# Hybrid encoder layer: another order and other places for the input norm, the Hyena projections, the filter network and the spectra

## The chip, the cores and the metric

One core of a Trainium2 chip runs the whole layer in one launch. The metric is device microseconds of that core. TensorE is called PE here, VectorE DVE, ScalarE ACT, GpSimd POOL; SyncE (SP) issues nearly all DMAs. Each engine works through its own queue in order, and engines wait for each other with semaphores.

## What is computed

A normed input of 1024 tokens by 1024 channels is projected once, and three mixers (Hyena, RG-LRU, latent attention) share the columns. The change touches the input norm, the projection and the Hyena mixer:

```python
x = _layer_norm(x, ln_in_g, ln_in_b)
proj = x @ w_in[l]
p_hy, p_lr, p_lg, p_cq, p_ckv, p_kr = jnp.split(proj, IN_SPLITS, axis=-1)
...
u = _depthwise_conv(u, conv_w, conv_b, 1, 1)          # width 3
x1, x2, v = jnp.split(u, 3, axis=-1)
h = sin(f1 * (z @ w1 + b1)); h = sin(f2 * (h @ w2 + b2))
h = (h @ w3).reshape(length, 2, 2, 256) * window      # taps of the long filters
z = v
for o, gate in enumerate((x1, x2)):
    z = gate * (_bidir_fftconv(z, h[:, 0, o], h[:, 1, o]) + skip[o] * z)
```

Behind it stand the attention, the output projection, a norm, an expert-choice mixture of 16 experts and a last norm. All products here are float32.

## The kernel before

Everything is written out by hand: one block of code per engine, semaphores between them, and fixed word addresses in one on-chip array (`mem(at, ...)`). So the order of the work is the order of the source, and what may be loaded when follows from which buffers lie on top of each other.

The **front** runs as follows. SP loads three tiles of x (128 tokens each), then twenty small parameter loads and the window table `win`; a further tile is loaded into one of three buffers when the old one is stored and turned (L408 to L412). DVE takes statistics and norms a tile (L1454 to L1460), PE turns it with 8 transposes (`x_turn`, L983), ACT copies it with gain and offset into `xT` (L657). Between the tiles stand the filter network: two small layers (L995, L999) with DVE's argument reduction (`sine_args`, L1445 to L1450) and ACT's sine (L646), then eight tap steps (L1010) of two 64-row matmuls each, whose products DVE multiplies with the window (L1486) and POOL folds into sums and differences (L519, L520). Then PE makes the filter **spectra**: four groups of 16 matmuls with the tables `fc` and `fs` (L1026); ACT copies half of each (L683, L684) and DVE combines them (L1498 to L1502, semaphore `spectra_done`).

Next come the six Hyena **projections** of 16 matmuls (`project`, L1042). ACT applies the centre tap of the short convolution (L697), DVE the outer ones (L1515 to L1519), PE turns the result (`hy_turn`, L1054), ACT and DVE copy it (L689, L1507). DVE folds (L1535, L1536), and the **convolution** `conv(0)` begins: spectrum matmuls with `dc` and `ds` (L1077), products on DVE, inverse matmuls with `ic` and `is_` (L1087, L1088). Project 6 stands between `conv(0)` and `conv(1)`, projects 7 to 9 behind it; then PE turns Hyena's result back (L1106, semaphore `hyena_back_psum`), does project 10 and begins the RG-LRU gates (L1120), which need 16 small weights.

**SP's queue** behind the front: `win_w` chunks 0 to 2 when `fc` and `fs` have landed; the four convolution tables and `skipb` when the spectra are done; chunks 3 and 4; then, when the second convolution's inverse sums are in PSUM (`inverse_psum`), 16 loads of the attention's weights (`wq`, `wqr`, `wk`, `wv`; 128 or 256 KB each), three rope loads (1,088 KB together), chunk 5, the 16 loads of the gates' weights (16 KB each, L449), and the last chunks. The loads from `wq` to the gates' weights are 4.8 MB without chunk 5.

The functions follow with their line numbers.

Of the kernel before, what the change touches and what calls it, by code (L numbers as in the profile page):

```python
# [80 lines left out]
def encoder(nc, A, out):  # L81

    ctx = ExitStack()
    with ctx:
# [74 lines left out]
        xT = mem(9168, KT, T)  # L159
        fc, fs = mem(17360, 8, HALF), mem(21456, 8, HALF)  # L160
        hf = mem(25552, 8, 2, HALF)
        pos_t, w3 = mem(39888, T, p1=POS), mem(40912, 1024, p1=FFN)
        h1, h2 = mem(41936, T, p1=FFN), mem(42960, T, p1=FFN)
        win = mem(43984, 8, HYW)
        xr_in = mem(46032, 3, D)
        hw = mem(49104, 2, 1024)
        fodd = mem(51152, 2, HALF)
        warg, turns = mem(52176, T, p1=FFN), mem(24528, T, p1=FFN)
# [4 lines left out]
        ic, is_ = mem(25552, 8, HALF), mem(29648, 8, HALF)  # L173
        pm = mem(39888, 2, 4, HYW)
        zbuf = mem(41936, 4, 2, HYW)
        yf = mem(43984, 2, HALF)
        t1, t2 = mem(45008, HALF), mem(45520, HALF)
        odd = t1[:, 0:HYW]
        skipb = mem(52176, 2, HYW)
        tsk = mem(37840, 4, 2, HYW)  # L180
# [64 lines left out]
        s_tab, s_par, s_wint, s_fmat = sem("tables_ld"), sem("params_ld"), sem("window_ld"), sem("filter_mats_ld")  # L245
        s_x = [sem(f"x_ld{i}") for i in range(3)]
# [66 lines left out]
        def reverse(m, a, b):  # L313

            return u_hy[:, m, T - 1 - a:T - 1 - b:-1]
# [66 lines left out]
        def _(sp):  # L382
# [22 lines left out]
            sp.dma_start(win, rows(A["c_win"])).then_inc(s_wint, 16)  # L405
            for i in range(TT):
                sp.wait_ge(s_xn, i + 1)
                sp.dma_start(xh_tok[:, i, :], xr_in[:, i % 3, :]).then_inc(s_xst, 16)  # L408
                if i + 3 < TT:
                    sp.wait_ge(s_xst, 16 * (i + 1))  # L410
                    sp.wait_ge(s_xp, i + 1)
                    sp.dma_start(xr_in[:, i % 3, :], x_tok[:, i + 3, :]).then_inc(s_x[i % 3], 16)  # L412
                if i == TT - 4:
                    sp.dma_start(fc, rows(A["c_fc"])).then_inc(s_fmat, 16)
                    sp.dma_start(fs, rows(A["c_fs"])).then_inc(s_fmat, 16)
# [8 lines left out]
            for c in range(3):  # L424
                load_w(c)
# [1468 lines left out]
```

## Time and profile before

| | us |
|---|---|
| median of 3 runs | 1700.0 (1694.19 to 1701.23) |
| the profiled execution, its own time | 1701.48 |
| its span, first to last instruction | 1699.4 |
| first convolution matmul starts | 234.46 |
| first gate matmul starts | 418.51 |

The profile is one execution. In the timeline a row gives start, duration, engine, source line, operation, output and input, a count, and in brackets how long the engine sat idle and what released it. A float32 matmul leaves two records on PE. PEld rows are its weight loads; on SPq a row is the issue of a DMA, not its transfer. PEclk in the table by stretch is TensorE's granted clock as a share of 2.4 GHz.

### The profile page before, as it was taken

Reading aid. Unit: us, or ns where it says so; the run is one execution under the profiler, and the core shown is the slowest. Engines: PE = TensorE matmul, PEld = TensorE weight load, DVE = VectorE, ACT = ScalarE, POOL = GpSimd, SP = SyncE. Lnnn points to the kernel's source line nnn. Section 1 sums busy time; section 2 is a strip of 40 time slices with the busy share of each in tenths; the row PEclk is TensorE's granted clock in tenths of the full one; section 3 lists DMA queues with packets and bytes.
Section 4 is the critical chain, followed back from the end, with each engine's and each line's share of the span. In section 5 each row is a group of like instructions: output and inputs, shape, how many; then the busy total and the mean of one; then the engine's idle time right before and its main releaser. Section 6 shows DMA issues by size and latency. Waiting matters only on the chain.

```text
span 1699.4 us, 15517 instructions
## 1 busy us (share of the span) xinstructions
PE 1571.0 (92%) x5758; PEld 1047.3 (62%) x5758; DVE 1050.5 (62%) x1024; ACT 722.7 (43%) x720; POOL 351.1 (21%) x190
## 2 busy tenths in 40 slices
PE   5999989999989999999998997099999999999997
PEld 2444458764334444555555886078888888888774
DVE  6311243551532346467766564869999998999886
ACT  5201100021432211434443143067777777777773
POOL 0400000000000000314446341403322342224304
PEclk9999989999999999999999998589999999999999
DMA  5605100052100000000012235869999999999995
GB/s 187 223 0 217 36 0 1 0 93 73 44 6 0 0 0 0 25 1 21 5 37 88 81 118 177 306 236 367 379 369 379 378 379 368 379 379 378 379 370 212
DMA packets 152852, 284.40 MB, mean 167 GB/s; under 512 B 25268, under 2 KB 35842, under 8 KB 152803
## 3 DMA queue, kind: packets, MB, share of 16 engines
q1 hardware_dynamic: 147187, 263.28, 43.7%
q0 software_dynamic: 4464, 16.25, 3.6%
q10 hardware_dynamic: 1152, 4.19, 0.6%
q8 instruction: 33, 0.54, 0.1%
q14 instruction: 16, 0.13, 0.0%
HBM read 259.07 MB, written 24.64 MB: 167 GB/s over the span
## 4 chain that ended last, share of the span: by engine, by line
PE 83%; DVE 7%; ACT 4%; DMA 4%; issue 2%; POOL 0%; POOLq 0%; ACTq 0%; SPq 0%; DVEq 0%
PE psum L1042 16%; PE psum L1391 9%; PE psum L1393 9%; PE psum L1392 9%; PE psum L1269 6%; PE psum L1205 4%; PE psum L1077 3%; PE psum L1026 3%; DMA arena<-in_exp_w_down 3%; PE psum L1175 2%; PE psum L1315 2%; PE psum L1317 2%; PE psum L1316 2%; PE psum L1088 2%; PE psum L1087 2%
## 5 line engine op out<-in xcount | busy, mean ns | idle before, releaser
L1815 DVE TENSOR_TENSOR split_at<-arena,split_at 128x2048 fp32r<-128x2048 f32 x188 | 427.6, 2290 | 61.8 <-ACT split_at L921 60.0
L921 ACT ACTIVATE split_at<-arena 128x2048 fp32r<-128x2048 f32 x192 | 367.5, 1916 | 64.2 <-PE psum L1393 54.1
L1391 PE MATMUL psum<-split_at,split_at 128*128 128x512 f32 x768 | 306.4, 399 | 1.4 <-DVE split_at L1821 1.4
L1393 PE MATMUL psum<-split_at,split_at 128*128 128x512 f32 x768 | 300.6, 391 | 0.0
L1392 PE MATMUL psum<-split_at,split_at 128*128 128x512 f32 x768 | 299.9, 391 | 0.0
L1042 PE MATMUL psum<-arena 128*128 128x512 f32 (+1 forms) x608 | 267.0, 598 | 3.7 <-DVE arena L1502 3.7
L1042 PEld LDWEIGHTS psum<-arena 128*128 128x128 f32 (+1 forms) x608 | 113.9, 188 | 152.4 <-issue 147.8
L1393 PEld LDWEIGHTS psum<-split_at,split_at 128*128 128x128 f32 x768 | 144.8, 189 | 31.4
L1391 PEld LDWEIGHTS psum<-split_at,split_at 128*128 128x128 f32 x768 | 145.0, 189 | 29.8 <-DVE split_at L1821 1.8
L1392 PEld LDWEIGHTS psum<-split_at,split_at 128*128 128x128 f32 x768 | 145.2, 189 | 28.4
L1269 PE MATMUL psum<-arena 128*128 128x512 f32 x256 | 120.8, 594 | 6.2 <-ACT arena L830 5.4
L820 ACT ACTIVATE arena<-psum 128x1024 f32<-128x1024 f32 x64 | 65.3, 1021 | 134.7 <-PE psum L1257 134.6
L1677 DVE TENSOR_REDUCE arena<-psum 128x1 f32<-128x1024 f32 x64 | 78.1, 1224 | 59.1 <-PE psum L1175 59.0
L593 POOL COPY arena<-arena 128x1 uint32 (+1 forms) x16 | 28.7, 1792 | 381.5 <-DVE arena L1849 360.3
L1205 PE MATMUL psum<-arena 128*128 128x512 f32 x176 | 77.0, 592 | 0.0
L1269 PEld LDWEIGHTS psum<-arena 128*128 128x128 f32 x256 | 47.2, 189 | 44.8 <-issue 39.1
L926 ACT ACTIVATE split_at<-psum 128x512 fp32r<-128x512 f32 x64 | 38.2, 597 | 81.8 <-PE psum L1360 68.2
L1719 DVE RECIPROCAL arena<-arena 64x256 f32<-64x256 f32 x32 | 55.9, 1748 | 21.8 <-ACT arena L830 20.9
L543 POOL MEMSET arena<- 128x2048 f32 x1 | 1.8, 1811 | 310.5 <-PE psum L1205 310.5
L1077 PE MATMUL psum<-arena 128*128 128x256 f32 x256 | 60.7, 394 | 3.4 <-DVE arena L1536 3.4
L1619 DVE TENSOR_SCALAR arena<-psum,arena 128x1024 f32<-128x1024 f32 x8 | 10.3, 1284 | 85.0 <-ACT arena L759 85.0
L1255 PE MATMUL psum<-split_at,split_at 104*128 104x512 f32 x128 | 62.2, 486 | 0.0
(282 smaller groups left out, 2235.8 us busy)
## 6 DMA issues: line engine op xcount, KB each, us to landing
arena<-in_exp_w_gate SPq DMA_DIRECT2D x64, 1024.0 KB, 14.2
arena<-in_exp_w_up SPq DMA_DIRECT2D x64, 1024.0 KB, 14.1
arena<-in_exp_w_down SPq DMA_DIRECT2D x64, 1024.0 KB, 14.2
arena<-in_w_in SPq DMA_DIRECT2D x9, 1024.0 KB, 5.4
arena<-in_x SPq DMA_DIRECT2D x8, 512.0 KB, 4.1
xhat_scratch<-arena SPq DMA_DIRECT2D x8, 512.0 KB, 6.1
arena<-in_w_out SPq DMA_DIRECT2D x8, 512.0 KB, 3.6
arena<-xhat_scratch SPq DMA_DIRECT2D x8, 512.0 KB, 4.9
```

What stands on the lines that cost most here:

```text
L820: a(p_at[:, n % 2, :], bank(2 * (n % 2), 2), ACT.Exp).then_inc(s_exp, 1)
L921: a(flat(wsplit[c % WS][0]), wraw[:, c], ACT.Copy).then_inc(s_whi, 1)
L1042: ins = mm(bank(proj_bank(i) + j, 1, p0, p0 + w), win_w[:, c % 3, k, at:at + w], xT[:, k, HALF * j:HALF * j + HALF], start=(k == 0), stop= ...
L1077: ins = mm(bank(4 + f % 2)[:, HYW * part:HYW * part + HYW], mat[:, i, P * f:P * f + P], pm[:, part, i, :], start=(i == 0), stop=(i == 3))
L1205: ins = mm(bank(heads_bank(u) + j), w[:, k, P * i:P * i + P], src[:, k, HALF * j:HALF * j + HALF], start=(k == 0), stop=(k == n_k - 1))
L1255: mm(out_, k[0][0:DR1, kc], q[0][0:DR1, qc], start=True, stop=False)
L1269: ins = mm(bank(6 + j), v1[:, h % 2, kb, :], p_at[:, n % 2, HALF * j:HALF * j + HALF], start=(kb == 0), stop=(kb == TT - 1))
L1391: mm(bank(out_bank), src[0][:, k, :], whi[:, k % 4, :], start=(k == 0), stop=False)
L1392: mm(bank(out_bank), src[0][:, k, :], wlo[:, k % 4, :], start=False, stop=False)
L1393: ins = mm(bank(out_bank), src[1][:, k, :], whi[:, k % 4, :], start=False, stop=(k == KT - 1))
L1677: v.tensor_reduce(nm[:, h % 2, qt:qt + 1], bank(b, 2), AX.X, ALU.max, negate=True).then_inc(s_nm, 1)
L1815: tt(flat(lo), wraw[:, c], flat(hi), ALU.subtract).then_inc(s_wlo, 1)
```

## The change

Four things are moved.

1. **Buffers.** All eight tiles of x have a place of their own (`xr_in` holds 8); the filter network's buffers move; `u_hy` shrinks from six columns to two; `dc`, `ds_`, `ic`, `is_`, `zbuf`, `tsk`, `yf`, `t1` and `t2` move; the ten weight chunks get fixed places. `zbuf` and `tsk` (words 25552 to 29647) now lie under `wq` (from 26576).
2. **SP.** The window is now the 21st load that PE waits for ahead of the parameter turns. All x tiles and chunks 0 to 2 are issued at once, the stores of the normed tiles after them. `fc`, `fs` and `skipb` follow, `dc` after four projections, `ds_` when the taps are folded, `ic` and `is_` in two parts behind the spectra (parts of 2 and 6 of 8 groups). Chunk 5 comes before the attention's weights. These wait for `hyena_back_psum` and `proj_psum`.
3. **PE, with ACT and DVE to match.** Four tiles are turned, then half of project 0 (its first 512 tokens) is done, then the other tiles and halves; filter layers and tap steps stand between the projections, each tap step in banks 6 and 7; the spectra come last, and then `conv(0)`. ACT copies pairs of tiles, 256 columns at a time. DVE takes the statistics of a tile ahead of the norm of the one before.
4. **DVE in the convolution.** The fold of `conv(0)` stands ahead of the spectra's combination; the skip product moves from the start to f = 3.

Core of the diff:

```diff
-        xr_in = mem(46032, 3, D)
-        win_w = mem(33744, 3, KT, 256)
-        u_hy = mem(39888, 6, T)
-        dc, ds_ = mem(17360, 4, T), mem(21456, 4, T)
-        zbuf = mem(41936, 4, 2, HYW)
-        tsk = mem(37840, 4, 2, HYW)
+        xr_in = mem(17360, TT, D)
+        u_hy = mem(41936, 2, T)
+        ic, is_ = mem(17360, 8, HALF), mem(21456, 8, HALF)
+        dc, ds_ = mem(33744, 4, T), mem(37840, 4, T)
+        zbuf, tsk = mem(25552, 4, 2, HYW), mem(27600, 4, 2, HYW)
...
-            sp.dma_start(win, rows(A["c_win"])).then_inc(s_wint, 16)
+            sp.dma_start(win, rows(A["c_win"])).then_inc(s_par, 16)
+            sp.dma_start(xr_in[:, 3, :], x_tok[:, 3, :]).then_inc(s_x[3], 16)
+            load_w(0)
+            for i in range(4, TT):
+                sp.wait_ge(s_x[i % 4], 16)
+                sp.dma_start(xr_in[:, i, :], x_tok[:, i, :]).then_inc(s_x[i % 4], 16)
+            load_w(1)
+            load_w(2)
...
-            sp.wait_ge(s_inv, 8)
+            sp.wait_ge(s_hyT, 2)
+            sp.wait_ge(s_pj, 10)
             for dst, name, n_k, d0 in ((wq, "mla_w_uq", 6, 0), (wqr, "mla_w_uq", 6, DV), (wk, "mla_w_ukv", 2, 0), (wv, "mla_w_ukv", 2, DV)):
...
-            pe.wait_ge(s_par, 16 * 20)
+            pe.wait_ge(s_par, 16 * 21)
...
+            def project_half(i, j):
+                ...
+                for k in range(KT):
+                    if i == 0:
+                        pe.wait_ge(s_xT, 8 + k + 1 + 16 * j)
+                    ins = mm(bank(proj_bank(i) + j), win_w[c][:, k, at:at + P], xT[:, k, HALF * j:HALF * j + HALF], start=(k == 0), stop=(k == KT - 1))
+                return ins
...
+            def window(nt):
                 v.wait_ge(s_f3, nt + 1)
...
+            sine_args(0)
+            hy_taps(0)
+            hy_taps(1)
+            sine_args(1)
...
+                elif f == 0:
+                    pe.wait_ge(s_kf, 16)
```

The first place is PE's queue from the second pair of tiles on. L983 (L995 in the changed code) are the input turns, L995, L999 (L1024) the filter layers, L1010 the tap steps, L1014 the half projections. Before:

```order
L990 MATMUL psum<-arena 128x78 [waits params_ld]
L991 MATMUL psum<-arena 64x4
L995 MATMUL psum<-arena 64x512 [waits params_copied]
L995 MATMUL psum<-arena 64x512
L983 MATMUL psum<-arena 128x128 [waits xT_done,in_normed]
L983 MATMUL psum<-arena 128x128 x7
L999 MATMUL psum<-arena 64x512 [waits sine_done] x2
L983 MATMUL psum<-arena 128x128 [waits xT_done,in_normed]
L983 MATMUL psum<-arena 128x128 x7
L1010 MATMUL psum<-arena 128x512 [waits sine_done]
L1010 MATMUL psum<-arena 128x512
```

After, from the same parameter turns on:

```order
L1001 MATMUL psum<-arena 128x78 [waits params_ld]
L1002 MATMUL psum<-arena 64x4
L995 MATMUL psum<-arena 128x128 [waits in_normed]
L995 MATMUL psum<-arena 128x128 x7
L995 MATMUL psum<-arena 128x128 [waits xT_done,in_normed]
L995 MATMUL psum<-arena 128x128 x7
L995 MATMUL psum<-arena 128x128 [waits in_normed]
L995 MATMUL psum<-arena 128x128 x7
L1014 MATMUL psum<-arena 128x512 [waits xT_done,w_in_ld0,params_copied]
L1014 MATMUL psum<-arena 128x512 [waits xT_done] x7
L995 MATMUL psum<-arena 128x128 [waits xT_done,in_normed]
```

The layers and the tap steps left this place, and half of a projection stands ahead of tile 4.

The second place is PE's queue behind project 5. In the changed code L1063 is a projection, L1075 a Hyena turn, L1036 a tap step, L1047 the spectra. Before, from the last turn (L1054) to the convolution (L1077 and behind):

```order
L1054 MATMUL psum<-arena 128x128 x3
L1054 MATMUL psum<-arena 128x128 [waits hyena_copied_dve]
L1054 MATMUL psum<-arena 128x128 x3
L1077 MATMUL psum<-arena 128x256 [waits hyena_copied_dve,hyena_copied_act,folded,dft_ld,proj_read_act]
L1077 MATMUL psum<-arena 128x256 x15
L1087 MATMUL psum<-arena 128x256 [waits product_done]
L1088 MATMUL psum<-arena 128x256
```

After, from the second half of turn 4, behind project 5:

```order
L1075 MATMUL psum<-arena 128x128 x3
L1036 MATMUL psum<-arena 128x512 [waits filter_windowed]
L1036 MATMUL psum<-arena 128x512
L1036 MATMUL psum<-arena 128x512 [waits filter_windowed]
L1036 MATMUL psum<-arena 128x512
L1036 MATMUL psum<-arena 128x512 [waits filter_windowed]
L1036 MATMUL psum<-arena 128x512
L1075 MATMUL psum<-arena 128x128 [waits hyena_copied_act,proj_read_dve]
L1075 MATMUL psum<-arena 128x128 x3
L1075 MATMUL psum<-arena 128x128 [waits hyena_copied_dve]
L1075 MATMUL psum<-arena 128x128 x3
L1047 MATMUL psum<-arena 128x512 [waits proj_read_dve,filter_folded,proj_read_act,filter_mats_ld]
```

The last three tap steps and the last turn stand there now, and the spectra behind them.

The third place is SP's queue around the attention's weights. Before:

```order
L421 DMA arena<-in_w_in 128x8x256 [waits proj_psum] x2
L438 DMA arena<-in_mla_w_uq 128x8x64 [waits inverse_psum]
L438 DMA arena<-in_mla_w_uq 128x8x64 x5
L438 DMA arena<-in_mla_w_uq 128x8x32 x6
L438 DMA arena<-in_mla_w_ukv 128x8x64 x4
L441 DMA arena<-in_c_rot 128x128 [waits z_done]
L441 DMA arena<-in_c_cos 128x1024
L441 DMA arena<-in_c_sin 128x1024
L421 DMA arena<-in_w_in 128x8x256 [waits proj_psum]
L449 DMA arena<-in_lru_wa 64x64 [waits zeroed]
L449 DMA arena<-in_lru_wa 64x64 x3
```

After:

```order
L408 DMA arena<-in_w_in 128x8x256 [waits spectrum_psum]
L448 DMA arena<-in_mla_w_uq 128x8x64 [waits proj_psum,hyena_back_psum]
L448 DMA arena<-in_mla_w_uq 128x8x64 x5
L448 DMA arena<-in_mla_w_uq 128x8x32 x6
L448 DMA arena<-in_mla_w_ukv 128x8x64 x4
L451 DMA arena<-in_c_rot 128x128 [waits z_done]
L451 DMA arena<-in_c_cos 128x1024
L451 DMA arena<-in_c_sin 128x1024
L458 DMA arena<-in_lru_wa 64x64 [waits zeroed]
L458 DMA arena<-in_lru_wa 64x64 x3
L458 DMA arena<-in_lru_wx 64x64 x4
```

Chunk 5 stands ahead of the block, and the block's first load waits for another semaphore.

## Rows read from the trace of the kernel before

**Rows 1.** The page's engine line: busy time, share, instructions.
```profile
PE 1571.0 (92%) x5758; PEld 1047.3 (62%) x5758; DVE 1050.5 (62%) x1024; ACT 722.7 (43%) x720; POOL 351.1 (21%) x190
```

**Rows 2.** Busy time by stretch, its first line names the columns.
```profile
core 0: us, PE busy (x) PEld busy (x) DVE busy (x) ACT busy (x) POOL busy (x), PEclk, DMA share, GB/s
...
9.84:74.78 64.94, 52.15 (x106) 23.93 (x107) 40.32 (x69) 32.22 (x79) 17.91 (x16) 1.00 0.72 239
...
136.34:234.46 98.12, 91.20 (x241) 42.59 (x241) 23.09 (x33) 11.70 (x18) 0.00 (x0) 0.95 0.28 102
234.46:361.83 127.37, 127.37 (x545) 105.60 (x546) 54.66 (x107) 3.12 (x6) 0.00 (x0) 0.98 0.00 1
```

**Rows 3.** Clock: a stretch's busy time, and timeline rows (start, duration, engine).
```profile
62.98 0.33 PEld L1010 LDWEIGHTS psum<-arena 64*128 64x128 f32 x1 [0.52 <-issue]
...
136.34:141.62 5.28, 5.28 (x6) 2.19 (x7) 0.00 (x0) 0.00 (x0) 0.00 (x0) 0.50 1.01 403
...
234.46 10.20 PE L1077 MATMUL psum<-arena 128*128 128x256 f32 x32 [3.37 <-DVE arena L1536]
...
306.57 7.07 PE L1077 MATMUL psum<-arena 128*128 128x256 f32 x32
```

**Rows 4.** DMA issues with time to landing, and the timeline's first 22 us.
```profile
arena<-in_c_win SPq DMA_DIRECT2D x1, 1024.0 KB, 6.4
...
9.91 0.59 SPq L405 DMA_DIRECT2D arena<-in_c_win  x1
...
15.56 5.68 ACT L657 ACTIVATE arena<-psum,arena 128x128 f32<-128x128 f32 x16 [1.29 <-DVE arena L1473]
...
17.66 0.80 DVE L1445 TENSOR_SCALAR arena<-psum,arena 64x512 f32<-64x512 f32 x1 [2.14 <-PE psum L995]
...
19.18 1.97 PE L983 MATMUL psum<-arena 128*128 128x128 f32 x8
...
21.18 0.80 DVE L1445 TENSOR_SCALAR arena<-psum,arena 64x512 f32<-64x512 f32 x1
```

**Rows 5.** Timeline: a window product, the spectra's end, the last projection's end.
```profile
66.62 1.23 DVE L1486 TENSOR_TENSOR arena<-psum,arena 128x1024 f32<-128x1024 f32 x1 [2.19 <-PE psum L1010]
...
132.69 0.60 ACT L683 ACTIVATE arena<-psum 128x512 f32<-128x512 f32 x1 [12.65 <-PE psum L1026]
...
136.34 30.36 PE L1042 MATMUL psum<-arena 128*128 128x512 f32 x64 [3.69 <-DVE arena L1502]
...
225.18 1.45 ACT L697 ACTIVATE arena<-psum,arena 128x512 f32<-128x512 f32 x2 [12.68 <-PE psum L1042]
...
229.56 1.52 PE L1054 MATMUL psum<-arena 128*128 128x128 f32 x8 [3.55 <-DVE arena L1519]
```

**Rows 6.** Timeline of SP's queue, and time to landing of its last two LRU loads.
```profile
362.02 11.78 SPq L438 DMA_DIRECT2D arena<-in_mla_w_uq  x12
...
379.99 0.43 SPq L421 DMA_DIRECT2D arena<-in_w_in  x1
380.85 2.44 SPq L449 DMA_DIRECT2D arena<-in_lru_wa  x4
...
388.45 3.54 SPq L449 DMA_DIRECT2D arena<-in_lru_wx  x4
...
DMA to landing us min/median/max: 2.0/2.6/3.2
```

**Rows 7.** Timeline of PE behind the second convolution.
```profile
403.03 1.91 PE L1106 MATMUL psum<-arena 128*128 128x128 f32 x16
404.77 13.90 PE L1042 MATMUL psum<-arena 128*128 128x512 f32 x32
418.51 1.88 PE L1120 MATMUL psum<-arena 128*128 128x512 f32 x4
423.08 1.98 PE L1120 MATMUL psum<-arena 128*128 128x512 f32 x4 [2.69 <-ACT arena L747]
...
446.71 2.95 PE L1129 MATMUL psum<-arena 128*128 128x512 f32 x4
```

More of the change, by code:

```diff
@@ new lines, in _ @@
+            sp.wait_ge(s_pj, 4)
+            sp.dma_start(dc, rows(A["c_dc"])).then_inc(s_dmat, 16)
+            sp.wait_ge(s_hab, 8)
+            sp.wait_ge(s_pj, 6)
+            sp.dma_start(ds_, rows(A["c_ds"])).then_inc(s_dmat, 16)
+            sp.wait_ge(s_dft, 4)
+            for part in range(2):
+                g = slice(2, 8) if part else slice(0, 2)
+                if part:
+                    sp.wait_ge(s_dmat, 48)
+                sp.dma_start(ic[:, g, :], rows(A["c_ic"])[:, g, :]).then_inc((s_fmat, s_dmat)[part], 16)
+                sp.dma_start(is_[:, g, :], rows(A["c_is"])[:, g, :]).then_inc((s_fmat, s_dmat)[part], 16)
@@ L441, in _ @@
                 sp.dma_start(dst, A[name]).then_inc(s_rope, 16)
-            load_w(5)
             sp.wait_ge(s_zero, 1)
@@ L650, in in_root @@
                 a(sd[:, i % 2:i % 2 + 1], mv[:, i % 2, 1:2], ACT.Sqrt, bias=eps).then_inc(s_sd, 1)
-            def x_copy(i):
-                act.wait_ge(s_xp, i + 1)
-                src = bank(4 + 2 * (i % 2), 2)
-                for k in range(KT):
-                    ins = a(xT[:, k, P * i:P * i + P], src[:, P * k:P * k + P], ACT.Identity,
-                            scale=par[:, C_LG + k:C_LG + k + 1], bias=par[:, C_LB + k:C_LB + k + 1])
-                ins.then_inc(s_xT, 1)
-            act.wait_ge(s_eps, 1)
@@ L662, in _, with x_copy @@
-            for i in range(3):
-                in_root(i)
-            act.wait_ge(s_parc, 2)
-            x_copy(0)
-            x_copy(1)
+            def x_copy(p, k):
+                if k == 0:
+                    act.wait_ge(s_xp, 2 * p + 2)
+                a(xT[:, k, 256 * p:256 * p + 256], bank(4 + k // 2)[:, 256 * (k % 2):256 * (k % 2) + 256], ACT.Identity,
+                  scale=par[:, C_LG + k:C_LG + k + 1], bias=par[:, C_LB + k:C_LB + k + 1]).then_inc(s_xT, 1)
+            act.wait_ge(s_eps, 1)
@@ new lines, in _, with hy_copy @@
+            in_root(0)
+            in_root(1)
+            act.wait_ge(s_parc, 1)
+            for p in range(TT // 2):
+                for half in range(2):
+                    if 2 * p + 2 + half < TT:
+                        in_root(2 * p + 2 + half)
+                    for k in range(4 * half, 4 * half + 4):
+                        x_copy(p, k)
+            def hy_copy(m):
+                act.wait_ge(s_ut, 2 * m + 1)
+                a(g_hy[:, m // 2, :, 0, P * (m % 2):P * (m % 2) + P],
+                  bank(4).rearrange("p (i c) -> p i c", i=4), ACT.Copy).then_inc(s_uta, 1)
@@ L667, in _, with hy_centre @@
+            def hy_centre(m):
+                act.wait_ge(s_pj, m + 1)
+                if m >= 2:
+                    act.wait_ge(s_ut, 2 * m - 2)
+                y = bank(proj_bank(m), 2)
+                for dst, src in ((u_hy[:, m % 2, 0:HALF], y[:, HALF:]), (reverse(m, 0, HALF), y[:, 0:HALF])):
+                    ins = a(dst, src, ACT.Identity, scale=par[:, C_HYW + 6 + m:C_HYW + 7 + m], bias=par[:, C_HYB + m:C_HYB + m + 1])
+                ins.then_inc(s_pja, 1)
             sines(0)
-            in_root(3)
```

276 lines of the change are left out of this document (151 added, 125 removed).

## The prediction

> **What bounds the kernel now.** I read the page's engine line first: PE is busy 92% of the span [rows 1]. Then the table by stretch [rows 2]. From the first convolution matmul (234.46 us) to the projections behind the second convolution (361.83) PE is busy 127.37 of 127.37 us, so whatever start the convolution is given is passed on whole to what follows. Ahead of it PE is not full: 52.15 of 64.94 us in the first stretch, 91.20 of 98.12 in the projections. The end is set by PE's in-order queue, and the change is worth two numbers: how much earlier than 234.46 the convolution starts, and whether a wait of PE behind it gets longer.
>
> The clock comes next [rows 3]. A float32 matmul leaves two records. At the 2.4 GHz level a 512-column record costs 0.43 us (32 of them, one projection, take 404.77 to 418.51, 13.7 us [rows 7]); after the wait at 132 to 136 us the granted clock is 0.50, the 1.2 GHz level, and six records take 5.28 us where six at the higher level take 2.6: a **cold start costs 2.6 us**. The same block of 32 convolution records takes 10.20 us cold and 7.07 warm, so 3.1 there. The filter's 64-row matmuls at 62.98 repeat every 0.33 + 0.52 = 0.85 us, the low level too, although the granted clock reads 1.00 there: the column seems to know nothing before its first event. Waits of PE fall on both sides: after 2.69 us four records took 1.98 us, still fast, a later four took 2.95 [rows 7].
>
> **The change, part by part. First half: the front.** All PE work ahead of the convolution stays the same; only order and waits change. I walk the new order with durations of the old trace.
>
> *To the first half projection.* Tiles 0 to 2 come as before, and x_turn(0) too. But PE now turns the parameters ahead of x_turn(1) and waits for 21 loads with the window among them: issued 9.91, landing 6.4 us later, 16.3 [rows 4]. The two small turns end at 17.0, tile 1's turns (8 records 1.97 us cold) at 18.9. ACT's copies are now 8 of 256 columns a pair. Before, 16 of 128 columns took 5.68, 0.36 each; a 512-column one with scale and bias takes 0.73 (two lie in the 4.38 us below). I take 0.45 as nearer the narrow one, 3.6 a pair plus 0.3 for a root; the ends 2.8 and 5.8 stay for the range. Copies end 22.8, tiles 2 and 3 are turned at 26.6 (tile 4's load, behind the first weight chunk, is near 22 at the 403 GB/s of [rows 3] and just keeps up), and the first half projection starts at **27.2**.
>
> *Two projections.* 16 records, 6.9 us, and a cold start: 36.7. Tiles 4 and 5: 38.5. PE waits 4.1 for copies, turns 6 and 7 cold: 46.1. Three more halves 20.6, the first filter layer 1.7, a cold start 2.6: 71.0; second layer 72.8. project(2) needs bank 0 read: DVE's sine argument takes 3.52 a half (17.66 to 21.18 [rows 4]), two halves behind the first layer end at 70.5, then ACT's centre tap and DVE's four taps take 4.38 (225.18 to 229.56 [rows 5]): **75.7**, a PE wait of 3 us.
>
> *Four projections with the taps between.* Projections 4 x 13.7 = 54.9. The eight tap steps now share one pair of banks, so each following step waits for DVE's window product, 1.23 [rows 5] and some 0.3 of semaphores: 1.5 us. Group after project(2): two turns, two steps, one wait, and the second turn's wait for copies: 7.3. After project(3): 5.8. After project(4): 2.6. After project(5) DVE's queue holds taps(5) ahead of window(5): 4.4 + 1.3, and then two steps of 1.7, a wait of 1.5 and the last turn: 11.9. Spectra can start at 75.7 + 54.9 + 27.6 = **158.2**.
>
> *Spectra and hand-over.* 128 records 54.9, cold start 2.6: 215.7. The hand-over of the spectra to DVE cost PE 3.7 us before (132.69 to 136.34 [rows 5]); it is no longer followed by a projection but by the convolution, which waits for the same spectra_done. So the old taps-and-fold wait, 3.55 + 3.4, goes, and this one takes its place: convolution at **219.4** if the clock falls nowhere else. The tables are early: dc after project(3), ds at the last fold some 50 us ahead; ic and is, in two parts behind the spectra, have 3.7 + 10 us for 1 MB and then 14 more for 3 MB. The skip product that moves to f = 3 (2.29 us on DVE) lies in DVE's wait for PE.
>
> *The clock in the groups.* They are stretches of turns, 64-row matmuls and waits. If it falls in all of them: three more cold starts, 7.8, and 8.6 for small matmuls at half speed, 16.4; if nowhere, 0. The trace shows 64-row matmuls never raising it and waits of 3.4 us and more ending cold, so I take a bit over half, 9. Convolution at 228.4, the **front gives 6 us** (range -1 to 15).
>
> **Second half: the SP queue behind the convolution.** The scratch of the convolution (zbuf, tsk) now lies where wq is loaded, so SP waits for hyena_back_psum, PE's last Hyena turn, where it waited for inverse_psum. Behind that wait stand, in order, 16 MLA loads, 3 rope loads and 16 LRU gate loads. Before, the block ran from 362.02 to 391.99 [rows 6] under two projections. Its last loads are needed by the first gate matmul, 418.51, which followed the turns (403.03 + 1.91 = 404.94) by one projection, 13.6 us [rows 7]. SP's issue alone, without load_w(5) that is gone from it (0.43 and the gap of 0.43 behind it), is 29.97 - 0.86 = 29.1 us; the last load is issued 0.6 ahead of the end and lands 2.0 to 3.2 later: 30.5 to 31.7. So the gate matmul could start at 435.5 to 436.7 on the old scale: PE waits 17.0 to 18.3 us where it waited nothing; I take **17.7**. Nothing on PE can pass it; the gates' own waits for ACT start from the matmul and move along.
>
> The clock falls in such a wait. Eight gate records at half speed cost 3.4 and the next projection's start 2.6: 6.0 at most; if the clock is back after the first part, 2.6. I take **4.3**.
>
> Sum: -6.0 + 17.7 + 4.3 = **+16 us**. The profiled execution (1701.48, span 1699.4) would become 1717.5, the median of the runs, 1700.0, **1716**.
>
> **A rule weighed.** LRU loads of 16 KB are issued every 0.6 us (four in 2.44) and MLA loads every 0.98 [rows 6]. The Trainium skill, "DMA: Bandwidth & Descriptors", section "Issuing engines are not separate DMA queues", holds that starting a DMA is usually small next to the DMA itself. By that rule the block would be bound by its 4.8 MB; the rows speak against it for loads this small.
>
> **The rivals.**
> 1. *Loads hidden after all, faster.* If the block ran at the 403 GB/s that the large loads reach [rows 3], its 4.8 MB took 11.9 us and landed some 14 us after the turns, when the gates want it. Stall and restart vanish, the front's 6 remain: 1694. Against: SP's rows are 0.6 and 0.98 apart whatever they carry. Chance 0.04.
> 2. *Front at its best, about the same.* The clock falls in no group and copies are cheap: -12 to -15, then +17.0 and +2.6 to +4: 1704 to 1708. Even then the front must reach the convolution by 234.5 - 22 = 212.5 to pay, and the walk's 219.4 without extra falls is above it. Chance 0.12.
> 3. *Front slower too, more than forecast.* All groups cold, the copies at their dear end (twice 2 us): the convolution starts at or after 234.5: 0 or more, 18.3 and 6: 1724 to 1730. Chance 0.12.
> 4. *The order doesn't act* (window or chunk 0 lands late, so the halves wait as the tiles did): front 0 to 3, the stall stays: 1720 to 1723, inside the forecast's range.
>
> **How the numbers follow.** Forecast with rival 4: 0.72, 1709 to 1724. Rivals 0.04, 0.12, 0.12. A measurement of this kernel tells about 0.5%, 8.5 us, from no change. Faster 0.04; same 0.14 (rival 2 and the forecast's lower edge); slower 0.82. Range **1703 to 1726**: best front with cheapest restart (-15 + 17.0 + 2.6 = +4.6, less run spread) to the dear end (+1 + 18.3 + 6 = +25).
>
> **What would show it.** In the changed profile: the first half projection near 27, spectra from about 158 to 172, the first convolution matmul at 219 to 235; MLA loads issued only after the last Hyena turn; the gate matmul with 17 to 18 us idle ahead, granted clock 0.5 behind it. I am wrong if that idle is below 10 us, if the convolution starts before 212, or if a new wait for ic or is stands at the first inverse matmuls.

## The result, and the profile after

The changed kernel takes **1711.5 us** (median; runs 1709.0 to 1714.2) against 1699.0 us of the kernel before (1694.2 to 1701.2). One more run, 2872.3 us at a mean granted clock of 0.56, was in a slow state and is left out of the spread and the ratio, though not of the median. The ratio is 1.0079, 95% interval 1.0061 to 1.0097. That is 12.5 us slower, where 16 were forecast (1716, range 1703 to 1726).

The profiled execution took 1713.9 us, its span 1711.8, which is 12.4 us over the span before. PE's queue sets the end here as before, so the two timelines can be laid side by side. This is PE's timeline of the changed kernel: start, duration, engine and line, operation, count, and in brackets the wait ahead of the row and what ended it.

```profile
16.03 0.39 PE L1001 MATMUL psum<-arena 78*128 78x78 f32 x1 [4.83 <-DMA arena<-in_c_win]
...
26.98 7.10 PE L1014 MATMUL psum<-arena 128*128 128x512 f32 x16 [0.75 <-ACT arena L667]
...
39.95 3.09 PE L995 MATMUL psum<-arena 128*128 128x128 f32 x16 [4.12 <-ACT arena L667]
...
70.55 15.67 PE L1063 MATMUL psum<-arena 128*128 128x512 f32 x32 [2.47 <-DVE arena L1555]
...
118.29 16.06 PE L1063 MATMUL psum<-arena 128*128 128x512 f32 x32
...
156.62 3.78 PE L1036 MATMUL psum<-arena 64*128 64x512 f32 x4 [2.77 <-DVE arena L1535]
...
165.43 1.97 PE L1075 MATMUL psum<-arena 128*128 128x128 f32 x8
167.19 56.63 PE L1047 MATMUL psum<-arena 128*128 128x512 f32 x128
227.59 8.83 PE L1120 MATMUL psum<-arena 128*128 128x256 f32 x32 [3.78 <-DVE arena L1596]
...
394.80 1.91 PE L1152 MATMUL psum<-arena 128*128 128x128 f32 x16
396.54 13.90 PE L1063 MATMUL psum<-arena 128*128 128x512 f32 x32
426.92 3.78 PE L1166 MATMUL psum<-arena 128*128 128x512 f32 x4 [16.48 <-DMA arena<-in_lru_wx]
433.40 3.51 PE L1166 MATMUL psum<-arena 128*128 128x512 f32 x4 [2.69 <-ACT arena L758]
436.74 13.90 PE L1063 MATMUL psum<-arena 128*128 128x512 f32 x32
...
461.43 27.85 PE L1063 MATMUL psum<-arena 128*32 128x512 f32 x64
```

Read it from the two places that the prediction named. The first convolution matmul (L1120, L1077 before) starts at 227.59 where it started at 234.46 [rows 3]: the front gives 6.9 us. The first gate matmul (L1166, L1120 before) follows its projection after 16.48 us idle; in [rows 7] it followed at once. Behind it the gate records take 3.78 us for four where they took 1.88, which is the 1.2 GHz level against 2.4 (the granted clock of these 3.78 us is 0.50, that of the 1.9 us before is 1.00). (Rows of 95.46, 15.53 us, and 137.07, 14.00 us, for project(3) and (5) are left out.) From the first gate matmul to the projection with 32 rows of output (461.43 here, 449.59 before) it is 34.5 us where it was 31.1: a restart of 3.4 us.

The account in differences of span, from the timelines: convolution start -6.9, its first block -1.4 (8.83 against 10.20), wait +16.5, restart +3.4, all the rest +0.8; together +12.4.

SP's queue shows why PE waits:

```profile
396.74 11.85 SPq L448 DMA_DIRECT2D arena<-in_mla_w_uq  x12
408.62 4.11 SPq L448 DMA_DIRECT2D arena<-in_mla_w_ukv  x4
...
415.29 2.42 SPq L458 DMA_DIRECT2D arena<-in_lru_wa  x4
...
422.88 2.51 SPq L458 DMA_DIRECT2D arena<-in_lru_wx  x4
```

The first two rows are the attention's 16 loads, called MLA loads in what follows. The block is issued from 396.74, at the last Hyena turn's end, and not from under the two projections ahead of it as in [rows 6]. The sixteen gate loads stand at its end; the last of them is issued at 424.8 and PE goes on at 426.9.

By stretch, with the columns of [rows 2] (busy time of each engine, then granted clock, DMA share, GB/s):

```profile
9.27:70.55 61.28, 44.99 (x139) 24.44 (x139) 24.62 (x51) 21.55 (x45) 0.00 (x0) 0.97 0.72 258
70.55:167.19 96.64, 89.58 (x209) 39.43 (x210) 33.32 (x45) 10.20 (x16) 18.28 (x16) 0.86 0.06 22
167.19:227.59 60.40, 56.62 (x129) 24.73 (x129) 13.93 (x19) 4.34 (x8) 2.14 (x2) 0.97 0.14 48
227.59:353.60 126.01, 126.01 (x545) 104.62 (x546) 54.71 (x107) 3.12 (x6) 0.00 (x0) 0.99 0.16 53
```

The second line is the four projections with the taps between them: 7.1 us of idle PE and a granted clock of 0.86, the only stretch of the front below 0.97. From the convolution on PE is full, as before. PE's waits for ACT's copies and for DVE's window products, in the first 480 us (sum, count, longest):

```profile
PE psum L995 <- ACT arena L667: 8.2, 2, 4.1
PE psum L1036 <- DVE arena L1535: 6.7, 4, 2.8
```

### The profile page after: what moved, and what is told of

Its sections match the earlier page's. It is cut to its first block, busy times and chain, and to the rows that moved or that the text cites. A ratio compares the mean times of both kernels' runs of the same rounds, so it can differ in the third digit from the quotient of the medians.

```text
span 1711.8 us, 15486 instructions
## 1 busy us (share of the span) xinstructions
PE 1563.2 (91%) x5758; PEld 1044.0 (61%) x5758; DVE 1049.9 (61%) x1024; ACT 712.0 (42%) x686; POOL 351.0 (21%) x190
## 4 chain that ended last, share of the span: by engine, by line
PE 80%; DVE 6%; DMA 5%; ACT 4%; issue 2%; SPq 2%; POOL 0%; POOLq 0%; ACTq 0%; DVEq 0%
PE psum L1063 13%; PE psum L1437 8%; PE psum L1439 8%; PE psum L1438 8%; PE psum L1315 6%; DMA arena<-in_exp_w_down 4%; PE psum L1251 4%; PE psum L1120 3%; PE psum L1047 3%; PE psum L1221 2%; PE psum L1361 2%; PE psum L1363 2%; PE psum L1362 2%; PE psum L1135 2%; PE psum L1134 2%
## 5 line engine op out<-in xcount | busy, mean ns | idle before, releaser
L1063 PE MATMUL psum<-arena 128*128 128x512 f32 (+1 forms) x544 | 241.8, 604 | 2.5 <-DVE arena L1555 2.5
L1063 PEld LDWEIGHTS psum<-arena 128*128 128x128 f32 (+1 forms) x544 | 102.8, 190 | 141.6 <-issue 141.5
L604 POOL COPY arena<-arena 128x1 uint32 (+1 forms) x16 | 28.7, 1792 | 382.2 <-DVE arena L1922 361.0
L1792 DVE RECIPROCAL arena<-arena 64x256 f32<-64x256 f32 x32 | 55.9, 1748 | 21.8 <-ACT arena L841 20.9
L1120 PE MATMUL psum<-arena 128*128 128x256 f32 x256 | 59.3, 387 | 3.8 <-DVE arena L1596 3.8
```

The costliest lines, as they stand in the source:

```text
L1063: ins = mm(bank(proj_bank(i) + j, 1, p0, p0 + w), win_w[c][:, k, at:at + w], xT[:, k, HALF * j:HALF * j + HALF], start=(k == 0), stop=(k = ...
L1120: ins = mm(bank(4 + f % 2)[:, HYW * part:HYW * part + HYW], mat[:, i, P * f:P * f + P], pm[:, part, i, :], start=(i == 0), stop=(i == 3))
```

## The experiments

Two accounts of the loss are possible. One: the front is a gain, and SP's block of loads behind its new wait costs more than the front gives. The rival: the slower time comes from the front itself or from an interplay (the clock, the halves), and the wait at the gates is only where it shows. The first two runs take the change apart into these two parts. The kernel before was timed again beside each set of runs: 1699.8, 1700.0 and 1699.5 us.

### The front alone

The gate and rope loads are put ahead of the block that waits for the last Hyena turn; all else is the changed kernel.

```diff
             load_w(5)
-            sp.wait_ge(s_hyT, 2)
-            sp.wait_ge(s_pj, 10)
-            for dst, name, n_k, d0 in ((wq, "mla_w_uq", 6, 0), ...):
-                ...
             sp.wait_ge(s_z, 8)
             ... rope loads, then the 16 gate loads ...
+            sp.wait_ge(s_hyT, 2)
+            sp.wait_ge(s_pj, 10)
+            for dst, name, n_k, d0 in ((wq, "mla_w_uq", 6, 0), ...):
+                ...
```

> The changed kernel with one edit: the wait for the last Hyena turn and the 16 attention loads stand behind the rope and gate loads in SP's queue. Theory (queue order): the gate weights are issued when the second convolution's results are done, land some 30 us before the gates, the 16.5 us wait of PE ahead of the first gate matmul is 0 and the 3.4 us of its cold start go with it: 1711.5 - 19.9 = 1691.6 us. Rival (the wait is only handed on): chunks 6 and 7, now behind the 16 attention loads, or the value weights come late and PE waits there for 5 to 16 us: 1697 to 1708. Rival (the wait has another cause than the order of the queue): no change, 1711.

Measured: 1689.0 us (1688.7 to 1692.9), ratio to the kernel before 0.9934, interval 0.9918 to 0.9951. Its PE timeline:

```profile
225.87 8.83 PE L1120 MATMUL psum<-arena 128*128 128x256 f32 x32 [3.78 <-DVE arena L1596]
...
408.55 1.88 PE L1166 MATMUL psum<-arena 128*128 128x512 f32 x4
413.12 3.01 PE L1166 MATMUL psum<-arena 128*128 128x512 f32 x4 [2.69 <-ACT arena L758]
...
439.64 27.85 PE L1063 MATMUL psum<-arena 128*32 128x512 f32 x64
```

The gate matmul follows its projection at once, at 2.4 GHz, and from it to the 32-row projection it is 31.1 us again. The front alone makes the kernel 10.7 us faster: 8.6 in the convolution's start, 1.4 in its first block. Against the changed kernel the 32-row projection comes 21.8 us earlier: 16.5 of wait, 3.4 of restart, and 1.7 by which this run's convolution started earlier with the same front.

### The queue alone

The mirror image: the kernel before, with its block of MLA, rope and gate loads put behind the wait for the last Hyena turn.

```diff
-            sp.wait_ge(s_inv, 8)
+            sp.wait_ge(s_z, 8)
+            load_w(5)
+            sp.wait_ge(s_hyT, 2)
+            sp.wait_ge(s_pj, 10)
             for dst, name, n_k, d0 in ((wq, "mla_w_uq", 6, 0), ...):
                 ...
-            load_w(5)
```

> The kernel before with its front untouched; only SP's queue is changed as in the changed kernel: chunk 5 first, then the wait for the last Hyena turn, then the 16 attention loads, rope and gate loads. Theory (queue order): the same wait ahead of the first gate matmul, 16.5 us, and 3.4 us of cold start, with no gain from the front: 1699.0 + 19.9 = 1718.9 us. Rival (the wait needs the new buffers or the new front): same as before, 1699.

Measured: 1717.7 us (1717.5 to 1718.5), ratio 1.0105, interval 1.0088 to 1.0122: 17.9 us slower than the kernel before. PE's timeline:

```profile
234.35 8.65 PE L1079 MATMUL psum<-arena 128*128 128x256 f32 x32 [3.37 <-DVE arena L1538]
...
433.12 3.78 PE L1122 MATMUL psum<-arena 128*128 128x512 f32 x4 [16.10 <-DMA arena<-in_lru_wx]
...
467.38 27.85 PE L1044 MATMUL psum<-arena 128*32 128x512 f32 x64
```

The old front and its convolution start (234.35, before 234.46) are untouched, and the wait of 16.1 us is there, with 34.3 us behind it where there were 31.1. In the four kernels the two parts add: -10.7 and +17.9 are +7.2, where +12.5 was measured for both. The traces show no interplay of the two in this gap of 5.3 us: the wait is 16.1 and 16.5 and the restart 3.2 and 3.4 with either front. In the profiled executions, at the 32-row projection, the parts sum to +7.8 (-9.95 and +17.8) and both together give +11.8. Of these 4.0 us, 1.7 are the same front's convolution start at 225.87 in one run and 227.59 in the other, 1.5 are that this kernel too ran its first block faster than [rows 3] (8.65 against 10.20), so that this gain is in the sum twice, 0.6 the wait and the restart. The other 1.3 us of the medians' gap no trace accounts for. The rival falls: the loss is the queue's, and it needs nothing of the front.

### What in the block costs the time

Three small kernels, all from the changed one. First, the sixteen gate loads of 16 KB made into eight of 32 KB, the same bytes:

```diff
-                    for c in range(2):
-                        for b in range(2):
-                            sp.dma_start(lruw[64 * b:64 * b + 64, 4 * d + 2 * g + c, 64 * b:64 * b + 64],
-                                         A[name][0, d, 2 * c + b]).then_inc(s_lw, 16)
+                    for b in range(2):
+                        sp.dma_start(lruw[64 * b:64 * b + 64, 4 * d + 2 * g:4 * d + 2 * g + 2, 64 * b:64 * b + 64],
+                                     A[name][0, d].rearrange("(c b) i j -> b i c j", b=2)[b]).then_inc(s_lw, 16)
```

> The changed kernel with the gates' weights loaded by 8 DMAs of 32 KB, not 16 of 16 KB. Theory (SP's issue bounds the block, 0.62 us a load): 8 issues fewer, the wait ahead of the gates falls from 16.5 to about 11.5 us, 1706.5 us. Rival (bytes bound the block): the same bytes, wait stays at 16.5.

One run: 1705.7 us. Two rows of SP's timeline, and PE's at the first gate matmul:

```profile
413.34 1.30 SPq L457 DMA_DIRECT2D arena<-in_lru_wa  x2
414.68 1.25 SPq L457 DMA_DIRECT2D arena<-in_lru_wx  x2
...
420.12 3.60 PE L1165 MATMUL psum<-arena 128*128 128x512 f32 x4 [11.62 <-DMA arena<-in_lru_wx]
```

A load of twice the bytes is issued in the same 0.63 us, and the wait of PE falls from 16.48 to 11.62, by 4.9 us for eight loads less (8 x 0.63 = 5.0). For the gate loads SP's issue is the price, and bytes are not.

Then the same question for the MLA loads: each cut into two of half the heads, 32 loads with the bytes and the pieces of the 16. A piece is a run of bytes that lie together in memory. Each whole load has 1024 of them (128 partitions x 8 heads), of 256 bytes in the loads of 256 KB and of 128 bytes in those of 128 KB, and not of 512 and 256, as the text below has it.

```diff
-                    sp.dma_start(dst[:, k, :].rearrange("p (h n) -> p h n", h=NH), src).then_inc(s_mw, 16)
+                    for h in range(0, NH, NH // 2):
+                        sp.dma_start(dst[:, k, :].rearrange("p (h n) -> p h n", h=NH)[:, h:h + NH // 2, :],
+                                     src[:, h:h + NH // 2, :]).then_inc(s_mw, 16)
```

> The changed kernel with each of the 16 MLA loads cut into two of half the heads: the same bytes and the same pieces of 256 and 512 bytes, in 32 loads instead of 16. It tells what the 0.98 us apart is that the MLA loads are issued at. Theory (SP pays by the load, whatever it carries): 16 more loads of 0.98, the block 15.7 us longer, PE waits 32 us at the first gate matmul, the time about 1726. Rival one (the time goes by the pieces that a load describes, or by the DMA engines that the block keeps at nine tenths busy): a half load takes 0.49, the block and the wait of 16.5 stay, 1711. Rival two (half loads cost what the small gate loads do, 0.62): the block 4 us longer, the wait 20.6, 1715.

One run: 1713.6 us. SP's timeline, and two windows, the first over most of the MLA loads, the second over halves of 64 KB alone (last columns: clock, DMA share, GB/s):

```profile
397.66 13.37 SPq L449 DMA_DIRECT2D arena<-in_mla_w_uq  x24
411.07 4.35 SPq L449 DMA_DIRECT2D arena<-in_mla_w_ukv  x8
...
398.70:415.40 16.70, 12.66 (x30) 5.32 (x28) 1.28 (x1) 1.22 (x2) 0.00 (x0) 1.00 0.97 184
406.50:411.00 4.50, 4.50 (x12) 1.88 (x10) 0.00 (x0) 0.00 (x0) 0.00 (x0) 1.00 0.72 112
```

A half load takes 0.56 us where a whole one took 0.98; 32 of them take 17.8 us where 16 took 16.0, and PE's wait is 17.1. The first theory (0.98 for each load, whatever it carries) falls; rival one is nearly right. With half of the pieces a load takes little more than half the time, and bytes are not what counts, since whole loads of 128 KB and of 256 KB both took about 0.98 us. What sets the pace is told in part. The twelve halves of 64 KB were still issued every 0.58 us while the 16 DMA engines were at a share of 0.72, so there the engines had room and SP's issue was the limit. With whole loads the share stands above 1 throughout (1.33 from 398.70 to 412.80 in the changed kernel), and there the two were not told apart. Cutting these loads gained nothing; joining them was not tried.

Last, the order inside the block, with the wait where it is: gate loads first, then rope, MLA last.

```diff
             sp.wait_ge(s_hyT, 2)
             sp.wait_ge(s_pj, 10)
-            ... 16 MLA loads, 3 rope loads, 16 gate loads
+            ... 16 gate loads, 3 rope loads, 16 MLA loads
```

> The changed kernel with the same wait ahead of SP's block behind the last Hyena turn, but inside the block the order is turned round: the 16 LRU gate loads first, then the 3 rope loads, the 16 MLA loads last. Theory (the price is where the gate weights stand in SP's queue, not the wait for the convolution's scratch in itself): the gates are issued from about 396 to 406 us, land by 409, one projection (13.7 us) ends at about 409 to 410, so PE waits 0 to 1 us where it waited 16.5, the restart goes too, and the time is 1689 to 1692, as with the block's gate loads moved ahead of the wait altogether (1689.0). The MLA weights then land near 430, about 10 us later than before, and their first matmul comes after 460. Rival (the block as a whole is late, the MLA weights or rope tables are wanted soon after): a new wait of PE for them, 5 to 10 us, and 1695 to 1702.

Measured: 1691.6 us (ten runs, 1689.2 to 1696.6), ratio 0.9956, interval 0.9944 to 0.9967.

```profile
394.93 2.39 SPq L449 DMA_DIRECT2D arena<-in_lru_wa  x4
...
402.48 2.51 SPq L449 DMA_DIRECT2D arena<-in_lru_wx  x4
...
408.47 1.88 PE L1166 MATMUL psum<-arena 128*128 128x512 f32 x4
```

The gates' loads are out by 405.0, under the projection that PE does meanwhile (394.73 to 408.47), and the gate matmul starts at 408.47 with no wait. No other wait for a load takes its place up to 640 us. So the wait for the convolution's scratch costs PE no wait in itself; the 16.5 us came from the order behind it, where the loads wanted first stood last. The median is 2.6 us above that of the front alone (1689.0). The two intervals just overlap and the two profiled executions are 0.2 us apart (1693.1 and 1692.9), so whether a small cost of the wait is left stays open.

### What bounds the front

The window's own semaphore: the parameter turns no longer wait for the window's 1 MB.

```diff
-            sp.dma_start(win, rows(A["c_win"])).then_inc(s_par, 16)
+            sp.dma_start(win, rows(A["c_win"])).then_inc(s_fmat, 16)
...
-            pe.wait_ge(s_par, 16 * 21)
+            pe.wait_ge(s_par, 16 * 20)
```

(The waits for `s_fmat` behind it count one load more, and DVE waits for it ahead of its first window product.)

> The changed kernel with the window's load taken out of what PE waits for ahead of the parameter turns (DVE waits for it at the first window product). Theory (that load sets the first half projection): parameter turns at 14.1 to 14.5 instead of 16.0, first half projection at about 25.2 instead of 27.0, convolution at 225.8 instead of 227.6, 1709.7 us. Rival (tile 4's load and DVE's norms set it): first half projection stays at 26.5 to 27.

One run: 1710.5 us. PE's rows, and DVE's first row on tile 4:

```profile
21.01 1.94 PE L995 MATMUL psum<-arena 128*128 128x128 f32 x8 [5.76 <-ACT arena L667]
23.92 1.97 PE L995 MATMUL psum<-arena 128*128 128x128 f32 x8 [0.97 <-DVE arena L1506]
...
21.46 0.70 DVE L1500 BATCH_NORM_STATS2 arena<-arena 128x6 f32<-128x512 f32 x1 [1.87 <-DMA arena<-in_x]
```

The parameter turns start at 12.82 where they started at 16.03, yet the first half projection starts at 26.64 (26.98) and the convolution at 228.34 (227.59). The rival is right, in its number and in its mechanism. DVE waits for tile 4's load until 21.46, takes that tile's statistics and only then norms tile 3 (from 23.05), and PE's turn of tile 3 waits for this norm. The 4.8 us at the window's load were covered by this chain.

The halves: in the front alone, the first half projection put behind the turns of all eight tiles.

```diff
-            project_half(0, 0)
             for i in range(TT // 2, TT):
                 x_turn(i)
+            project_half(0, 0)
```

> The changed front with the gate loads ahead, as in a1_gates_first, but the first half projection no longer stands between the turns of tiles 3 and 4: all eight tiles are turned first. Theory (the halves' head start is worth the PE work that it puts under the copies): PE waits for ACT's copies at each pair of tiles and has 7 to 9 us less to do there, the convolution starts 5 to 6 us later than 225.9, near 231, and the time is about 1694.6. Rival (copies and tile loads bound this stretch whatever PE does): the convolution is where it was, within 1.5 us, and the time 1689.

One run: the convolution starts at 232.10, 6.2 us later than 225.87, as the theory said (231). By the start of project(2) it is 3.9 us later (76.69 against 72.75), and this much is the wait that the half projection had covered. The other 2.3 us came in the groups behind it, whose code is the same: from project(2) to the spectra it is 96.2 us here and 93.1 in the front alone, but the changed kernel with the same code there took 96.6. So about 4 us are shown for the order, and the match with 231 is in part luck. The waits for ACT's copies are three of 4.1 us now, 12.3 in all, instead of two (8.2) with a half projection between them. The time, 1700.6 us, is some 6 us more than forecast; the profiled execution of the front alone took 1692.9, so like against like it is 7.7 more, and the 1.5 beyond the convolution's start are cold records behind the gates' waits for ACT.

The taps: in the front alone, extra matmuls that nothing reads, three and one of 512 columns, fill PE's waits ahead of tap steps 6 and 7.

```diff
-            for nt in range(5, 8):
-                taps_filter(nt)
+            taps_filter(5)
+            for nt in range(6, 8):
+                pe.wait_ge(s_pja, N_HY - 1)
+                pe.wait_ge(s_pjv, N_HY - 1)
+                for n in range((3, 1)[nt - 6]):
+                    mm(bank(0), win_w[2][:, 0, 0:P], xT[:, 0, 0:HALF], start=True, stop=True)
+                taps_filter(nt)
```

> As a1_gates_first, with extra work whose result nothing reads: three and one 512-column 128-row matmuls on an idle bank ahead of the last two tap steps, where PE only waited for DVE's window product. The waits for the window products stay as long in sum with the filler in them; only what the clock does can change. Theory (the clock is a cost of its own in these groups, beside the waits): tap steps 6 and 7 and the last Hyena turn run at the 2.4 GHz level (-4.5 us) and spectra start without a cold block (-1.7), so the convolution starts at 219 to 220 and the time is about 1683. Rival (only the waits count): the convolution stays at 225.9 or comes up to 1 us later, the time 1689 to 1690.

One run: 1690.3 us, the convolution at 224.54, where the theory said 219 to 220. PE's timeline:

```profile
156.68 2.84 PE L1097 MATMUL psum<-arena 128*128 128x512 f32 x6
159.53 1.98 PE L1036 MATMUL psum<-arena 64*128 64x512 f32 x4
161.44 1.12 PE L1097 MATMUL psum<-arena 128*128 128x512 f32 x2
162.82 1.98 PE L1036 MATMUL psum<-arena 64*128 64x512 f32 x4 [0.26 <-DVE arena L1540]
164.74 1.09 PE L1075 MATMUL psum<-arena 128*128 128x128 f32 x8
165.66 55.10 PE L1047 MATMUL psum<-arena 128*128 128x512 f32 x128
```

Here the theory holds step by step: both tap steps take 1.98 us instead of 3.78, the turn 1.09 instead of 1.97, the spectra 55.10 instead of 56.28. From project(5) to the spectra it is 25.7 us where it was 30.1 (165.81 - 135.69), and 1.2 more within the spectra: 5.6 us of the 6.2 forecast, for more work. The whole time doesn't show it, and it came out at the rival's number (1689 to 1690) for another reason. Earlier in this run project(3) took 16.17 us against 14.00 in the front alone, and project(4) 16.69 against 15.37, with the same code in both: 3.5 us given back, and 0.7 more lost ahead of project(2). That leaves about the 1.3 us by which the convolution came earlier than 225.87. So the clock is a cost beside the waits, and one filled wait doesn't settle the others.

The last run takes the waits away instead of filling them. The tap steps go inside the projections, one in project(2), two in project(3) and in project(4), three in project(5), each where DVE has long read the banks it needs; the last Hyena turn goes inside the first spectra; DVE's order follows.

```diff
+                    if k in steps:
+                        taps_filter(steps[k])
...
-            project(2)
+            project(2, {7: 0})
             hy_turn(0)
             hy_turn(1)
-            for nt in range(2):
-                taps_filter(nt)
-            project(3)
+            project(3, {2: 1, 6: 2})
...
+            project(4, {2: 3, 6: 4})
...
+            project(5, {1: 5, 4: 6, 7: 7})
...
-            hy_turn(5)
...
-            spectra(0)
+            spectra(0, True)
```

> The changed front with the gate loads ahead of the rotating block, as in a1_gates_first, and now the eight 64-row tap steps are put inside the projections (one in project(2), two in project(3), two in project(4), three in project(5)), each where DVE has long read the pair of banks it needs, and the last Hyena turn stands inside spectra(0). In a1_gates_first the convolution started at 225.9 us, PE waited 6.7 us in four places for window products, and several projections were entered from such waits at the lower clock level. Theory (waits for the window products and the clock that falls in the groups are what the front lost to its walk): both go, about 6.7 + 2.8 us of waits for copies and 9 us of clock, the convolution starts near 207, and the time falls from 1689 to about 1670. Rival (the 64-row matmuls bring the clock down wherever they stand, or ACT's and DVE's in-order queues turn the gained time into new waits for bank reads): the convolution at 212 to 217, the time 1676 to 1681. No gain at all would say that the groups' waits were hidden behind something else.

Measured: **1675.8 us** (1672.3 to 1677.6), ratio 0.986, interval 0.9843 to 0.9876: 24.2 us faster than the kernel before. Rows of PE's timeline, and the window from project(2) to the spectra:

```profile
70.36 13.95 PE L1070 MATMUL psum<-arena 128*128 128x512 f32 x28 [2.47 <-DVE arena L1554]
84.24 1.98 PE L1036 MATMUL psum<-arena 64*128 64x512 f32 x4
86.15 1.99 PE L1070 MATMUL psum<-arena 128*128 128x512 f32 x4
...
137.01 1.98 PE L1036 MATMUL psum<-arena 64*128 64x512 f32 x4
138.92 5.42 PE L1070 MATMUL psum<-arena 128*128 128x512 f32 x12
...
208.63 9.66 PE L1119 MATMUL psum<-arena 128*128 128x256 f32 x32 [3.78 <-DVE arena L1596]
...
70.36:148.87 78.51, 78.17 (x200) 33.92 (x201) 30.09 (x40) 8.33 (x13) 19.20 (x17) 0.98 0.07 27
```

All eight tap steps take 1.98 us, the projections run at the 2.4 GHz level but for the start of project(2) (granted clock 0.50 from 70.36 to 73.00), no wait for a window product is left, and the granted clock of the stretch is 0.98 where it was 0.86 in the changed kernel and 0.89 in the front alone. From project(2) to the spectra it is 78.5 us against 93.1 in the front alone (72.75 to 165.81), 1.0 of it moved into the spectra; the rest of the 17.2 us is 2.4 that this run was ahead at project(2). The convolution starts at 208.63, where the theory said 207 and the rival 212 to 217. The 2.4 us are no work of the edit (the first half projection took 7.11 us here and 9.27 there), and without them the start would be 211, between the two. It is the mechanism that decides: single steps of 64-row matmuls inside a projection did not bring the clock down, and no new wait for a bank came up. The time came 6 us above the 1670 forecast, at the rival's 1676: the profiled execution took 1672.3, the three others 1675.1 to 1677.6. What differs between them was not seen, since only one has a trace.

## Why the prediction was right

The verdict, slower by a small margin, was right, and both numbers it was built of were measured: the front -6 forecast, -6.9 read; SP's queue +22 forecast (17.7 and 4.3), +19.9 read. The median, 1711.5, lies 4.5 us under the forecast and well inside the range. In the profiled executions the gap is 3.6 us (+12.4 for +16): 0.9 of the front, 2.1 of the queue, 1.4 of the convolution's first block, which ran faster (8.83 for 10.20) and had no term in the sum, less 0.8 elsewhere.

**To the first half projection.** Parameter turns forecast 16.3, read 16.03; half projection 27.2, read 26.98. The reason given was the right one only in part: the run with the window's own semaphore moved the turns by 3.2 us and the half projection by 0.3. The chain there is tile 4's load, DVE's norm of tile 3 and ACT's copies, not the window.

**Two projections.** Forecast 75.7 for project(2), read 70.55. The cold start laid on the first half projection did not come in this run (7.10 us; 7.11 in the last experiment, 8.8 to 9.3 in the others with the same work up to there), and those laid on the halves and the second layer came to 0.6 together. The waits were as walked: 4.12 for copies (forecast 4.1), 2.47 for DVE's arguments and taps (3). ACT's price of 0.45 us for 256 columns stood.

**The groups.** Waits for window products forecast 1.5 us three times and a longer one, read 1.32 three times and 2.77. The clock took more than was taken: project(2), (3) and (4) took 15.67, 15.53 and 16.06 us, 5.6 over three of 13.9; four of the tap steps took 6.7 over 1.98 each; the last turn and the spectra 0.9 and 1.5 over 1.04 and 55.10. That is 14.7 us, of which the walk had 2.6 in the spectra's cold start and 9 in its allowance. From project(2) to the spectra 96.6 us went by where the walk had 82.5 and the allowance 9. The two errors, 5.1 us early at project(2) and 4.3 us late behind it, nearly cancel, which is luck: the convolution's 227.59 against 228.4 looks better than the working was. (One group of the walk doesn't add up either: the terms given for the one after project(5) make 11.5, not 11.9.)

**Spectra and hand-over.** Read 3.78 us at the convolution, forecast 3.7. Nothing waits for the tables.

**SP's queue.** Forecast 17.0 to 18.3 us of wait, 17.7 taken, read 16.48 and, with the old front, 16.10. The sum held: 16.0 for the MLA loads, 2.5 for rope and 10.1 for the gate loads, 28.7 where 29.1 was taken. The last loads landed in about 2.1 us, near the lower of the two ends. The restart was sized 4.3 and measured 3.4: eight gate records lost 3.4 together (3.78 and 3.51 here for 1.88 and 1.98), and the next projection started warm, where the dear end had 2.6.

**The rule weighed.** The Trainium skill, "DMA: Bandwidth & Descriptors", section "Issuing engines are not separate DMA queues", says that starting a DMA is usually small beside the DMA itself. For a single gate load the trace agrees: 0.63 us of issue, 2.1 to 2.6 us to landing. For sixteen in a row the rule misleads: the issues add up to 10.1 us while the landings overlap, the issue of 32 KB costs the same 0.63, and the wait falls with the number of loads. For the MLA loads the reading "whatever they carry" was the step that failed. 128 KB and 256 KB do cost the same, about 0.98 us, but they describe the same number of pieces; with half the pieces a load took 0.56. It did not change the sum, since the block was priced whole by its measured length.

**The rivals.** Loads hidden (1694): refuted by the 16.5 us, though the front alone, at 1689.0, shows what it would have been. Front at its best (1704 to 1708): the convolution would have had to start at 219.5 to 222.5. Front slower too: it never was; in seven profiles of this front, two of them with a small edit in it, the convolution started at 224.5 to 228.7. The order does act: the first half projection came at 27, and the run without it was 3.9 us behind at project(2). (That rival's own sum, a front of 0 to 3 with the stall of 22, gives 1719 to 1722, not 1720 to 1723.)

## What to carry to other kernels

Where a load is moved behind a later wait, price the whole block behind it in its queue, and put what is wanted first at its head: here that order alone was worth 20 us (1711.5 to 1691.6), with the wait left in place. Short matmul steps that wait for another engine cost twice here, by the wait and by the clock at 1.2 GHz after it; put inside a long run of matmuls, where the other engine has time to keep up, they cost only themselves. And when a change has a good and a bad half, run each half alone: the better kernel was one of the halves.

## What the runs showed of the hardware

- The same code with the same waits ran at different granted clocks in different runs: the first half projection took 7.10, 8.89, 9.07 and 9.27 us in four kernels whose PE work up to there is the same, and project(3) 14.00 in one and 15.5 to 16.2 in others. The convolution's start spread over 4.2 us (224.54 to 228.74) in seven profiles. From this spread an estimate: a walk of such a front can't be better than some 2 us to either side.
- The 64-row tap steps take 1.98 us at the 2.4 GHz level and 3.78 at the 1.2 GHz level. After a wait of 1.32 us they were seen at either (1.98 us at 93.89 and 3.78 at 113.90 in the front alone). Set inside projections they kept to 1.98. But they did not bring the clock up either: in the kernel before, from 35.83 to 73.4, tap steps and turns alternated with one wait of 1.08 us among them, and each of the eight steps took 3.5 to 3.8 us, the lower level.
- A gate load of 16 KB and one of 32 KB each took SP 0.63 us to issue, while a rope table of 512 KB took 0.43 and an MLA load of 128 or 256 KB 0.98. Bytes did not set these times. For the MLA loads the number of pieces did (0.56 with half of them, at a DMA share of 0.72 where the halves were of 64 KB); why a gate load, with 64 pieces, is dearer than a rope table was not tried. What stands ahead counts too: the rotation table of 64 KB took SP 0.34 and 0.58 us in the two kernels where no MLA load stood ahead of it, 0.50 behind the halves and 1.13 behind the whole MLA loads.
